# Two blocks on one core: the mask of the mLSTM recurrence on POOL, and the final norm of block 1 joined with the first adaptive norm of block 2

## The reference

```python
# block 1, mLSTM mixer, 4 heads, forward and backward: for query t and key s (s <= t, or s >= t backward)
# w[s, t] = exp(min(a[s] + m[t], 0)) * (k[s] . q[t])
# out[t] = sum_s w[s, t] v[s] / max(|sum_s w[s, t]|, thr[t])
...
# FNet mixer beside it: real part of a DFT over positions and channels, times fnet_w
...
h = rmsnorm(h, final_norm)                 # end of block 1
# block 2, each layer
mod = silu(c) @ ada_w[l] + ada_b[l]        # shifts, scales, gates
x = rmsnorm_2(h, norm_mix[l]) * (1 + sc_m) + sh_m
h = h + gt_m * hybrid_mixer(x, ...)
```

## Time and profile before

| | |
|---|---|
| median of 3 runs | 3979.68 us |
| the profiled execution | 3976.05 us |
| its span, first to last instruction | 3974.3 us |
| mean granted clock of PE | 0.956 |
| instructions | 42227 |

### The profile page before, as it was taken

How to read it: one execution, slowest core, us unless ns; L and a number is a source line. 1 busy time by engine, 2 the same in 40 slices (tenths; PEclk the granted TensorE clock), 3 DMA queues, 4 the chain that set the end, 5 groups by cost and what they waited for, 6 DMA issues and landing times. The chain is left out here.

```text
span 3974.3 us, 42227 instructions
## 1 busy us (share of the span) xinstructions
PE 3742.9 (94%) x16750; PEld 2885.9 (73%) x16750; DVE 2247.2 (57%) x3076; ACT 1276.4 (32%) x1827; POOL 659.3 (17%) x346
## 2 busy tenths in 40 slices
PE   8999997999999999987999979898999999989999
PEld 6888733788878888534888856686788777867887
DVE  6545555754564445457655575775544567755443
ACT  3222233522242223334422244334222343343221
POOL 3441000244214430000443102020000020200000
PEclk9999997999999999997999989898999998989999
DMA  4343200344323342101434212001222220012222
GB/s 167 137 138 105 89 23 5 131 135 135 119 96 124 133 139 86 57 23 56 140 136 139 94 62 71 17 1 54 80 97 98 85 77 24 1 39 86 98 97 80
DMA packets 92949, 345.44 MB, mean 87 GB/s; under 512 B 10833, under 2 KB 11089, under 8 KB 91857
## 3 DMA queue, kind: packets, MB, share of 16 engines
q1 hardware_dynamic: 92752, 342.74, 25.9%
HBM read 340.60 MB, written 2.10 MB: 86 GB/s over the span
## 5 line engine op out<-in xcount | busy, mean ns | idle before, releaser
L381 ACT ACTIVATE w_hi<-raw 128x1024 fp32r<-128x1024 f32 (+2 forms) x540 | 561.1, 1040 | 1919.7 <-PE ps L325 1906.0
L323 PE MATMUL ps<-xs_hi,w_hi 128*128 128x512 f32 x2472 | 980.1, 396 | 34.9 <-DVE xs_lo L538 14.5
L324 PE MATMUL ps<-xs_lo,w_hi 128*128 128x512 f32 x2472 | 970.0, 392 | 0.0
L325 PE MATMUL ps<-xs_hi,w_lo 128*128 128x512 f32 x2472 | 969.4, 392 | 0.0
L391 DVE TENSOR_TENSOR w_lo<-raw,w_hi 128x1024 fp32r<-128x1024 f32 (+2 forms) x540 | 669.0, 1240 | 128.5 <-ACT w_hi L381 128.3
L323 PEld LDWEIGHTS ps<-xs_hi,w_hi 128*128 128x128 f32 x2472 | 468.2, 189 | 158.9 <-issue 32.7
L776 POOL TENSOR_SCALAR arena<-arena,parg 128x768 f32<-128x768 f32 x128 | 304.5, 2390 | 1656.3 <-PE ps L325 910.1
L325 PEld LDWEIGHTS ps<-xs_hi,w_lo 128*128 128x128 f32 x2472 | 468.7, 190 | 99.1
L324 PEld LDWEIGHTS ps<-xs_lo,w_hi 128*128 128x128 f32 x2472 | 469.0, 190 | 98.1 <-issue 3.4
L323 PE MATMUL ps<-hd_hi,w_hi 128*128 128x512 f32 x1320 | 527.9, 400 | 4.6 <-DVE hd_lo L483 3.5
L324 PE MATMUL ps<-hd_lo,w_hi 128*128 128x512 f32 x1320 | 525.1, 398 | 0.0
(11 more groups left out here) (425 smaller groups left out, 4202.9 us busy)
## 6 DMA issues: line engine op xcount, KB each, us to landing
raw<-in_ffn_gu SPq DMA_DIRECT2D x264, 512.0 KB, 3.7
arena<-in_ada SPq DMA_DIRECT2D x64, 768.0 KB, 5.6
raw<-in_ffn_dn SPq DMA_DIRECT2D x96, 448.0 KB, 3.3
raw<-in_in_t SPq DMA_DIRECT2D x60, 512.0 KB, 3.6
raw<-in_ffn_dn SPq DMA_DIRECT2D x48, 512.0 KB, 3.5
raw<-in_out SPq DMA_DIRECT2D x32, 512.0 KB, 3.6
raw<-in_pleg SPq DMA_DIRECT2D x16, 512.0 KB, 3.6
raw<-in_in_r SPq DMA_DIRECT2D x8, 512.0 KB, 3.9
```

What stands on the lines that cost most here:

```text
L323: T.matmul(bank, lhs_hi(k), rhs_hi(k), start=(first and k == 0), stop=False)
L324: T.matmul(bank, lhs_hi(k), rhs_lo(k), start=False, stop=False)
L325: mm = T.matmul(bank, lhs_lo(k), rhs_hi(k), start=False, stop=(last and k == kt - 1))
L381: A.activation(self.hi[:, n % HL, 0:size], raw[:, n % RAW, 0:size], ACT.Copy).then_inc(self.high_done, 1)
```

## The change

In the recurrence stage:
- the mask moves from DVE to POOL, behind a semaphore of its own (weighted), and POOL's increment releases PE
- PE gets spreads 0 and 1 first, then four scores; the others two at a time in steps 0 and 1 and in step 3 of groups 0 to 3; the Fourier products of a group go before its steps 0, 1 and 2 (one, one, two); the next group's spread goes before step 1, the thresholds' before step 3
- each head's sums are evacuated by themselves, numerator and denominator have two buffers, and pair 2 accumulates in ps0 and ps1
- a division is split: the maximum on DVE in step 2 of the next pair, the reciprocal in four pieces of 128 columns in its steps 3 to 6, the multiplication (and addition) on POOL after its last mask; the last pair's stays on DVE whole.

At the end of block 1 FinalNorm no longer stands between GateEmbed and Project2. GateEmbed's emission squares h with a weight sqrt(g*g + eps) for each channel (g is the final gain) and multiplies by g times the adaptive gain; one root with eps squared as its bias stands for both norms. The stream itself is normalised within Project2.

```diff
+    class FinalShift(ShiftEmit):
...
+        def act_weights(self, act):
+            act.wait_ge(self.weights, 1)
+            A.activation(final_w, final_w, ACT.Sqrt).then_inc(self.weights, 1)
+
+        def dve_weights(self, dve, order):
...
+            V.memset(final_eps, EPS * EPS)
+            V.tensor_tensor(final_g, gain_m[0], g, ALU.mult)
+            order.done(V.tensor_tensor(final_w, g, g, ALU.mult))
+            V.tensor_scalar(final_w, final_w, EPS, None, ALU.add).then_inc(self.weights, 1)
+
+        def act(self, act, k):
+            if k == 0:
+                act.wait_ge(self.weights, 2)
+            A.activation(sq[:, k % 2, :], h[:, k, :], ACT.Square, scale=final_w[:, k:k + 1]).then_inc(self.squares, 1)
+            A.activation(self.whole[:, k, :], h[:, k, :], ACT.Copy, scale=self.gains[k])
+            if k >= 1:
+                act.wait_ge(self.added, k)
...
     class FinalNorm:
...
+        def act(self, act, j):
+            if 3 <= j <= 6:
+                for k in (2 * j - 6, 2 * j - 5):
...
+                    A.activation(head_sq[:, k % 4, :], h[:, k, :], ACT.Square).then_inc(self.squares, 1)
...
+            if j == 9:
+                act.wait_ge(self.summed, 1)
+                A.activation(rope_tmp, ps[5][:, :], ACT.Sqrt, scale=1.0 / D, bias=C("eps")).then_inc(self.rooted, 1)
+
+        def dve(self, dve, j):
+            if 4 <= j <= 7:
...
+                        V.tensor_tensor(hsq[:, :], hsq[:, :], head_sq[:, k % 4, :], ALU.add).then_inc(self.added, 1)
+            if j == 10:
+                dve.wait_ge(self.rooted, 1)
+                V.reciprocal(rope_tmp, rope_tmp).then_inc(self.inverted, 1)
+
+        def pe(self, pe, j):
+            if j == 8:
+                pe.wait_ge(self.added, DT)
+                T.matmul(ps[5][:, :], ones(P), hsq[:, :], start=True, stop=True).then_inc(self.summed, 1)
+
+        def pool(self, pool):
+            pool.wait_ge(self.inverted, 1)
             for k in range(DT):
...
+                G.tensor_scalar(h[:, k, :], h[:, k, :], col(0, cg, "final_norm", k), None, ALU.mult).then_inc(self.scaled, 1)
             for k in range(DT):
...
+                pool.wait_ge(self.scaled, k + 1)
+                G.tensor_tensor(h[:, k, :], h[:, k, :], rope_tmp, ALU.mult).then_inc(self.done, 1)
```

Project2 calls these by tile number j; its PE waits for the root before tile 10's row spreads, its DVE for all of POOL's (done) at tile 16, and POOL runs them behind its convolution. In the recurrence stage:

```diff
+                    q, k = g // 2, s_ % ST
+                    if s_ < 2:
+                        scores(pe, 4 + 2 * s_)
+                        scores(pe, 5 + 2 * s_)
+                    if k == 0:
+                        fourier(pe, g, 0)
+                    elif k == 1:
+                        if g < 6:
+                            fourier(pe, g, 1)
+                        if 1 <= g < 7:
+                            spread(pe, g + 1)
+                    elif k == 2:
+                        if g < 4:
+                            fourier(pe, g, 2)
+                            fourier(pe, g, 3)
+                    else:
+                        if g < 4:
+                            scores(pe, 8 + 2 * g)
+                            scores(pe, 9 + 2 * g)
...
+                    if k == 0:
+                        if q == 2:
+                            pe.wait_ge(qk_copied, 16)
+                        elif q:
+                            pe.wait_ge(evacuated, e + 1 if q == 1 else e + 3)
                     pe.wait_ge(wgt_ready, s_ + 1)
...
+                    if k == 1 and e == 0 and q:
+                        evacuate(act, q - 1, 1)
+                    if k == 2 and e == 1:
+                        evacuate(act, q, 0)
+                    if k == 3:
                         fourier_copy(act, g)
...
-                        order.done(V.tensor_tensor(wx[:, r], wx[:, r], qks[:, p, e, j, r], ALU.mult))
-                        dg = slice(j * P, (j + 1) * P)
-                        V.tensor_tensor(wx[:, dg], wx[:, dg], C("upto") if d == 0 else C("from"), ALU.mult) \
-                         .then_inc(wgt_ready, 1)
...
+                        V.tensor_tensor(wx[:, r], wx[:, r], qks[:, p, e, j, r], ALU.mult).then_inc(weighted, 1)
+                    q, i = divmod(s_, 2 * ST)
+                    if 1 <= q < NP and i == 2:
+                        bound(dve, order, q - 1)
+                    if 1 <= q < NP and 3 <= i <= 6:
+                        invert(dve, q - 1, slice((i - 3) * PIECE, (i - 2) * PIECE))
...
+            @st.block.gpsimd
+            def _(pool):
...
+                    pool.wait_ge(weighted, s_ + 1)
+                    G.tensor_tensor(wx, wx, C("upto") if d == 0 else C("from"), ALU.mult).then_inc(wgt_ready, 1)
+                    q, i = divmod(s_, 2 * ST)
+                    if q and i == 2 * ST - 1:
...
+                        pool.wait_ge(inverted, 4 * q + 4)
+                        if d == 0:
+                            G.tensor_tensor(hsum[:, p, :], nums[q % 2], dens[q % 2], ALU.mult).then_inc(dir_ready, 1)
```

More of the change, by code:

```diff
@@ L524, in act_finish @@
             act.wait_ge(self.sums, 1)
-            A.activation(root, ps[6][:, :], ACT.Sqrt, scale=1.0 / D, bias=C("eps")).then_inc(self.rooted, 1)
+            A.activation(root, ps[6][:, :], ACT.Sqrt, scale=1.0 / D, bias=self.bias()).then_inc(self.rooted, 1)
             for k in range(DT):
@@ L1661, in mixer1_mlstm @@
     def mixer1_mlstm(l, m, work, spectrum):
-        part, spec, dft, fw = spectrum
+        part, spec, second, dft, fw = spectrum
         y, cq, ckv, kr, mx, mo, gi, gf, vz, uq, ukv = m
@@ L1733, in scores_copy, with spread @@
                 A.activation(qks[:, m // 8, m % 2, m // 2 % ST, :], ps[m % 2][:, :], ACT.Copy).then_inc(qk_copied, 1)
+            def spread(pe, g):
+                p, d, e = groups[g]
+                if g >= 2:
+                    pe.wait_ge(arg_ready, ST * (g - 1))
+                T.matmul(ps[2 + g % 2][:, :], pick(36, 32 * d + 2 * p + e), rows_m[0:36, :], start=True, stop=True) \
+                 .then_inc(m_spread, 1)
             @st.block.tensor
             def _(pe):
-                for m in range(8):
+                for g in range(2):
+                    spread(pe, g)
+                for m in range(4):
                     scores(pe, m)
@@ new lines, in _, with bound @@
+                    if k == 3:
+                        fourier_copy(act, g)
+                evacuate(act, NP - 1, 1)
+            def bound(dve, order, q):
+                dve.wait_ge(evacuated, 2 * q + 2)
+                dve.wait_ge(thr_ready, q + 1)
+                order.done(V.scalar_tensor_tensor(out=larger, in0=dens[q % 2], scalar=-1.0, in1=thr[:, q % 2, :],
+                                                  op0=ALU.mult, op1=ALU.max))
+                V.tensor_tensor(dens[q % 2], dens[q % 2], larger, ALU.max).then_inc(bounded, 1)
+                dve.wait_ge(bounded, q + 1)
@@ L2104, in dve_after @@
                 self.win.dve_scale(dve, 4, 4)
+            if j == 16 and self.final:
+                dve.wait_ge(self.final.done, DT)
             for r in {16: (0, 1), 17: (2, 3), 18: (4,)}.get(j, ()):
@@ L2908, in _ @@
             ple.pe(pe)
-            final.pe(pe)
+            to_mix.pe(pe)
             proj.pe(pe)
@@ L2925, in _ @@
             modulation(dve, order)
+            to_mix.dve_weights(dve, order)
             ple.dve(dve)
-            final.dve(dve)
+            to_mix.dve_finish(dve)
             proj.dve(dve)
```

210 lines of the change are left out of this document (106 added, 104 removed).

## The result

The changed kernel takes 3914.33 us (median of 4, 3910.18 to 3916.69) against 3979.66: a ratio of 0.9833 (0.9816 to 0.985). Forecast were 3912 and a range of 3896 to 3936. Its profiled execution took 3916.69 us (span 3914.9), 59.4 less than that of before.

The account below looks back on a forecast made before the run. TensorE, busy 94% of the span, was taken as the bound. Two recurrence stages (51.8 us) and the norm (15.8) sum to 67.6 off 3976.05, giving 3908.4; with the median 3.6 higher, 3912, range 3896 to 3936.

Parts of the forecast that it names:

- start: Recurrence stage's opening, with the first product waiting for the DFT tables: no sooner than before, 9.2 us.
- Pair 0: First two groups of the recurrence stage: PE-bound, 16.7 us of work plus 3 for a possible lower clock, 19.7.
- Pair 1: Second two groups of the recurrence stage: PE-bound, nothing added since the wait for ACT's copies is gone, 16.7 us.
- Pair 2: Third two groups of the recurrence stage: DVE-bound, 13.0 us of work plus some 1.3 of POOL exclusion, 14.3.
- Pair 3: Last two groups of the recurrence stage: DVE-bound, 13.0 us of work plus some 1.3 of POOL exclusion, 14.3.
- the covered division: POOL's division before the next pair's first mask, 1.3 us (2.6 before the last pair): Fourier and spread products cover 1.8.
- The mask: Recurrence mask on POOL: 0.44 us each; 1.7 us a pair saved on DVE against 1.3 of exclusion, no real gain.
- The norm: Final norm at block 1's end: 16.8 us between two square roots removed, 1.0 added under Project2, net 15.8.
- Rival 1: Mask on POOL costs 1.08 us, DVE and POOL alternate: recurrence stage 90.8 us, total 3930; chance 0.12.
- Rival 2: PE's clock in the recurrence stage stays as mixed as before: 16 us more a stage, total 3944; chance 0.08.
- Rival 3: Short waits keep PE at 1.2 GHz throughout the recurrence stage: 121.4 us a stage, total 3991, slower; chance 0.03.
- Rival 4: Norm's join worth little: POOL delays DVE in Project2 by 5 us or more, or gate stage grows; 3918; chance 0.05.

Follow-up runs that it names:

- e1: Kernel before, with only the changed kernel's recurrence function and its second pair of evacuation buffers: 3930.9 us, ratio 0.9877.
- e8: Changed kernel plus a dummy square root before the gate stage's last emission, so the root's table loads early: 3919.4 us, ratio 0.9853.
- e12: The changed kernel measured again without any edit: 3924.3 us, ratio 0.9857.
- e2: Changed kernel with the old recurrence function put back, so only the norm's change remains: 3967.9 us, ratio 0.9969.
- e4: Kernel before with only the mask moved to POOL, old order kept: 3989.6 us, ratio 1.0027.
- e11: Changed kernel with divisions on DVE and the first group's Fourier products one step later: 3908.0 us, ratio 0.9818.
- e7: Changed kernel with each Fourier product of the first group issued one step later: 3914.3 us, ratio 0.9841.
- e5: Changed kernel with the divisions' multiplications and addition moved from POOL to DVE, after its seventh step of a pair: 3915.1 us, ratio 0.9840.
- e6: Changed kernel with divisions still on POOL but issued later, inside the next pair: 3910.5 us, ratio 0.9831.
- e3: Changed kernel with the mask back on DVE, new order kept and divisions still on POOL: 3917.5 us, ratio 0.9843.
- e10: Changed kernel with both mask and division on DVE, nothing on POOL in the stage: 3923.3 us, ratio 0.9862.
- e9: Changed kernel with POOL doing each mask twice: 3925.3 us, ratio 0.9862.

## Why the prediction was right

**The total.** 2.3 us off. Over the four kernels with the new stage unedited (changed, e1, e8, e12) it takes 82.6 us in the mean of eight, over before and e2 the old one 108.2 in the mean of four: 25.5 less a stage against 25.9 forecast. With the norm's 15.4, less 1.0 for the matrix sum under Project2, that is 65.5 of the 67.6. The profiled executions differ by 59.4: the changed kernel's own two stages take 4.0 more than that mean (47.1 won), and the unedited stretches took 2 more in all. How far these move is seen in block 2, which has 1618.0 to 1628.6 us in three kernels with the old norm (before, e1, e4), and 1620.2 to 1629.2 in eleven with the new. No trace of the kernel before could have told this beforehand, and the second measurement of the same kernel (3924.3) shows that the first one's closeness was partly luck; it too lies in the range.

**The stage, term by term** (forecast; first trace, e12, e11; the kernel before, cut alike, has 11.4, 23.4, 23.7, 23.9, 16.9 and 8.4): start 9.2; 10.8, 11.1, 7.6. Pair 0 19.7; 18.6, 18.6, 18.3. Pair 1 16.7; 17.5, 17.5, 17.5. Pair 2 14.3; 15.8, 15.8, 14.0. Pair 3 14.3; 14.1, 10.0, 11.3. Tail 7.6; 7.5, 7.5, 7.5.
- Start and pair 0 together were 28.9 and are 29.4 to 29.7. The Fourier product does begin at the tables' landing (588.76, 7.9 us after the issue), and there was a cold start (0.91). That this wait could be had back, by the order of three lines, I didn't see. The 9.2 was read up to the edge of a window at 590.0, not up to the first value product; and pair 0's sum leaves out the two score products of its step 1 (1.13): it takes 18.2 at full clock (e7, e11) where pair 1 takes 17.5.
- Pair 1 is bound by PE as forecast, 0.8 longer.
- **The step that failed** is the covered division: "2.6 ahead of pair 3; two Fourier and spread products cover 1.8". The code puts one Fourier product ahead of pair 3's first value product and the spread behind it, so PE had only the 1.0 us of L1770; DVE's multiplication was shut out besides (1.82 for 0.69), and PE waited 2.33. That is pair 2's 1.5 us, which e5, e6 and e11 give back (14.0 and 13.8, against 14.3 forecast).
- Pair 3's forecast was right by accident in the first trace: I had DVE as the bound at full clock, with 13.0 us of work, and it is 10.0 us at 1.00 with 8.7 us of DVE's work in it (e12). The 14.1 is PE at 0.55.
- What is open: no run separates the parts of the new order (the second buffers, the split evacuation, the divided reciprocal, the spread-out Fourier products), so how much each brings, and how much comes by the higher clock, is not shown.

**The mask** costs 0.46 us (0.44), minimum 0.41, two of 64 at 0.86. That the changed kernel's gain is the order's and not POOL's is shown twice, by e3 and e10. But the prediction's balance for the mask itself, 1.7 saved against 1.3 of exclusion, is not borne out: with nothing else on POOL it saves 1.6 in pair 2 at full clock (e10 against e5). By the Trainium skill (GPSIMD Engine Reference, Engine selection) elementwise work belongs on VectorE; e5 agrees for the division (0.69 us there, 1.27 to 1.60 on POOL). For the mask it is the other way round: 0.29 us on DVE and 0.46 on POOL, and yet the stage is 3.4 us shorter with it on POOL when POOL has nothing else (e5 against e10).

**The norm**: 15.4 for 16.8 (the reciprocal's 3.35 in that term stands in the earlier trace rows, not in the earlier trace rows). The failed sentence is "Its table load replaces the one before the norm's root". The weights' root took over the load of the gate norm's root (2237.86); a sigmoid's load follows (2242.49), and the last root needs its own, which stood hidden at 2333.68 before and now comes after the wait. The source has the wait ahead of the root in both kernels; why the load lay ahead of it in one and behind it in the other is open. e8 gives it back. For such a switch the Trainium skill (ScalarE: Activation LUTs, Rules for kernel authors) allows about 2.7 us; all loads of this case take 1.28, and e8 gained 1.3 by hiding one. Nobody waited for POOL's 25.3 us of work on the stream (eight scalings of 1.70, eight multiplications of 1.53, the last begun at 2391.8). And PE's wait for the l2 reciprocal is 0.8 us as before, so no exclusion was seen there. The 1.0 priced came as the matrix sum itself: L1304 takes 1.02 at 2346.11, and the offset to the kernel before falls by that much, from 63.8 to 62.7, and stays there up to 2397.

**The rivals.** Rival 1's mechanism was tried in e9: a step of about 1 us costs 3.6 us a stage and not 9. It had DVE and POOL alternate from pair 1 on, 18.1 us a pair: pair 2 took just that, but pair 1 hid the step (17.6) and pair 3, in which DVE has only 7.6 us of work up to the last value product, took 14.4 and 14.0 even at the lower clock. Rival 2's clock doesn't stay mixed: pairs 0 to 2 run at 0.91 to 1.00; it came true for pair 3, in some executions. The prediction's remark that 590 to 613 does not show swings of the clock claimed too much: 0.85 there means that three tenths of the stretch ran at the lower level. Rival 3 did not come. Rival 4's 5 us in block 2 can't be told from its unforced variation.

## What to carry to other kernels

When a stage alternates between engines, look first for the work that is ready and stands behind a wait in program order: the new order, with second buffers for the evacuation and a divided reciprocal, was worth 25 us a stage here. Moving the mask to another engine brought nothing that could be measured while long instructions shared its queue, and 3.4 us a stage once they were gone. Before giving a free engine a long instruction, look at which short one will stand behind it in its queue. Judge an edit of some us by the marks of its own stage, cut as finely as the edit (pair 2 was 15.8 in all eight unedited stages while the whole stage moved by 3.9 us), since the total can move by 10 us in stretches nobody touched.

## What the runs showed of the hardware

- After one and the same hole of 2.33 us, at the same place of the same code, PE's clock stayed at 1.00 in one execution and went to the lower level in another (0.55 over the next 14.1 us). Of the eight unedited stages one kept 1.00 in pair 3, the others had 0.70 to 0.54 and took 11.2 to 14.3 us for the 10.0; without the hole (e5, e11) all four stages kept 1.00. So a hole of 2.33 us can be followed by a loss of up to 4.3 more.
- A DVE multiplication that started together with a POOL multiplication of 1.27 us took 1.82, its own 0.69 and most of the other's; POOL's next took 1.60. It is what the earlier trace rows showed for a longer pair.
- Work taken off a busy engine made the whole slower (e4) though the stage got shorter, and the loss lay in stretches where PE ran the same products at a lower mean clock.
